# A two-block transformer forward pass on one core: the norm between MLP and attention is applied behind the first four projections

## The reference, cut to what matters

```python
# end of the first block
u = rms_norm(h, norm_mlp_pre[l])
f = jnp.square(jax.nn.relu(u @ w_mlp_in[l])) @ w_mlp_out[l]
h = h + rms_norm(f, norm_mlp_post[l])
# start of the second block, i = 0; x is h, ctx are 256 context tokens
hx = modulate(rms_norm_2(x, norm_g[i]), shift_x[:, None], scale_x[:, None])
hc = modulate(rms_norm_2(ctx, norm_g[i]), shift_c, scale_c)
#   rms_norm_2(x, g) = x * rsqrt(mean(x * x) + eps) * g;  modulate(h, shift, scale) = h * (1 + scale) + shift
qx, kx, vx, gx = split(hx @ w_in)       # w_in: 1024 -> 4 * 1024, 8 heads of 128
qc, kc, vc, gc = split(hc @ w_in)
qx = rope_axial(qx, ang_r, ang_c); kx = rope_axial(kx, ang_r, ang_c)
# per head: softmax(q1 k1) - lam * softmax(q2 k2), times v; then a norm, times silu(g)
```

## Time and profile before

| | us |
|---|---|
| median of 3 runs | 1629.29 (1629.1 to 1634.57) |
| the profiled execution, its own time | 1629.36 |
| its span in the profile | 1627.2 |
| outside the span | 2.16 |
| PE busy | 1556.7 (96% of the span) |
| DVE, ACT, POOL busy | 985.8, 751.7, 504.6 |
| mean granted clock of TensorE | 0.984 of full |

### The profile page before, as it was taken

The page is one execution under the profiler, slowest core; times in us unless marked ns, Lnnn a source line. Parts: engine busy times, 40 slices in busy tenths (PEclk is TensorE's granted clock), DMA queues, the critical chain, the costliest instruction groups (busy, mean ns, idle before and its releaser), DMA issues.

```text
span 1627.2 us, 23677 instructions
## 1 busy us (share of the span) xinstructions
PE 1556.7 (96%) x8392; PEld 1221.3 (75%) x8392; DVE 985.8 (61%) x2266; ACT 751.7 (46%) x1413; POOL 504.6 (31%) x231
## 2 busy tenths in 40 slices
PE   7998999999899999999899999999999989999997
PEld 5886666678688888888877877778777768876566
DVE  6235555355679867645666666675676267147854
ACT  6225766634342423234344554455445343248753
POOL 3651232245244444444221111121214354230012
PEclk9999999999999999999899999999999989999999
DMA  6861112264356565643111111111111122220001
GB/s 200 174 162 33 59 59 77 76 256 130 104 193 194 191 198 188 198 134 100 53 53 39 40 39 39 39 39 39 39 39 52 52 56 89 78 66 14 2 14 65
DMA packets 48401, 149.34 MB, mean 92 GB/s; under 512 B 5782, under 2 KB 9110, under 8 KB 48184
## 3 DMA queue, kind: packets, MB, share of 16 engines
q1 hardware_dynamic: 37080, 112.45, 23.0%
q10 hardware_dynamic: 11232, 35.72, 6.8%
HBM read 141.53 MB, written 6.62 MB: 91 GB/s over the span
## 4 chain that ended last, share of the span: by engine, by line
PE 80%; DVE 7%; ACT 5%; issue 5%; POOL 1%; DMA 1%; ACTq 0%; POOLq 0%; DVEq 0%; SPq 0%
PE ps L347 41%; PE ps L351 20%; PE ps L570 4%; PE ps L581 3%; PE ps L551 3%; PE ps L1347 3%; PE ps L1311 2%; PE ps L1323 1%; POOL w_l L973 1%; PE ps L415 1%; PE ps L1075 1%; ACT sb L636 1%; DVE tg L1921 1%; ACT w_h L330 1%; DVE b_sb L675 1%
## 5 line engine op out<-in xcount | busy, mean ns | idle before, releaser
L973 POOL TENSOR_TENSOR w_l<-raw,w_h 128x1024 fp32r<-128x1024 f32 (+1 forms) x190 | 457.0, 2406 | 897.1 <-ACT w_h L330 877.4
L330 ACT ACTIVATE w_h<-raw 128x1024 fp32r<-128x1024 f32 x190 | 200.7, 1058 | 360.5 <-PE ps L347 305.3
L347 PE MATMUL ps<-x2h,w_h 128*128 128x512 f32 (+1 forms) x816 | 245.3, 366 | 19.5 <-DVE x2l L1994 7.6
L347 PE MATMUL ps<-x1h,w_h 128*128 128x512 f32 x584 | 237.9, 407 | 16.0 <-POOL w_l L973 10.4
L347 PE MATMUL ps<-x2h,w_l 128*128 128x512 f32 (+1 forms) x816 | 231.8, 349 | 0.0
L351 PE MATMUL ps<-x2l,w_h 128*128 128x512 f32 (+1 forms) x816 | 231.7, 349 | 0.0
L347 PE MATMUL ps<-x1h,w_l 128*128 128x512 f32 x584 | 230.7, 395 | 0.0
L351 PE MATMUL ps<-x1l,w_h 128*128 128x512 f32 x584 | 230.1, 394 | 0.0
L347 PEld LDWEIGHTS ps<-x2h,w_h 128*128 128x128 f32 x816 | 132.4, 191 | 52.6 <-issue 17.1
L347 PEld LDWEIGHTS ps<-x2h,w_l 128*128 128x128 f32 x816 | 132.2, 191 | 20.8
L351 PEld LDWEIGHTS ps<-x2l,w_h 128*128 128x128 f32 x816 | 132.5, 191 | 19.5
(11 more groups left out here) (318 smaller groups left out, 2615.3 us busy)
## 6 DMA issues: line engine op xcount, KB each, us to landing
raw<-in_w_mlp SPq DMA_DIRECT2D x64, 512.0 KB, 3.7
mraw<-in_w_mod ACTq DMA_DIRECT2D x51, 512.0 KB, 3.7
raw<-in_w_a SPq DMA_DIRECT2D x32, 512.0 KB, 3.6
raw<-in_w_att SPq DMA_DIRECT2D x25, 512.0 KB, 11.3
raw<-in_w_b SPq DMA_DIRECT2D x20, 512.0 KB, 3.6
raw<-in_w_g SPq DMA_DIRECT2D x16, 512.0 KB, 3.6
raw<-in_w_ao SPq DMA_DIRECT2D x9, 512.0 KB, 3.5
gates<-g_stage ACTq DMA_DIRECT2D x16, 256.0 KB, 2.2
```

The lines of the kernel that those rows point to most:

```text
L330: nc.scalar.activation(split(u)[0], raw[:, u % RAW], ACT.Copy).then_inc(w_hi, 1)
L347: mm = nc.tensor.matmul(o, w[:, k], xh(k), start=(first and k == k0 and wi == 0), stop=(last and k == k1 - 1 and wi == 1))
L973: nc.gpsimd.tensor_tensor(l[:, ks], raw[:, u % RAW, ks], h[:, ks].bitcast(F32), ALU.subtract).then_inc(w_lo, 1)
```

## The change

Head 0's four projections are made from tiles of the residual stream that are multiplied by gain and scale only; the token's norm factor is applied to the finished PSUM banks, and the shift, which the norm factor doesn't touch, is added as a column.

- `x2h`/`x2l` get four more columns (SCX = SC + 4). Columns SC and SC+1 hold the two shift vectors, so `first_ctx` runs over C + 2 = 258 columns and its bank's column C is weight x shift. Addresses behind them move by a quarter KB.
- DVE's scale, add and low half of the unnormalised tile run together (`g_scale`, `g_add`, `g_low`), as in the kernel's norm ahead of the MLP (L1953, L1960, L1965). ACT rounds each tile to `xph` ahead of squaring it.
- PE: four k-tiles of context products of U_A between the steps of the first norm, the rest behind its spread, then all of U_A+1. Then for each of 8 tiles the column sums and the products of both units over the latent tokens. Then U_A+2: half, the second norm's spread, the other half, its context; then U_A+3, context and latent.
- U_A+2's weight has a third slot (`w_h4`/`w_l4`, over `m_l`), split behind the MLP, ahead of the first norm's root. U_A+3's weight is split behind the second spread, U_A+4's within the shifts at k = 3, U_A+5's behind the gate's tanh.
- DVE (`evict_first`) scales the shift column and multiplies the bank by the norm factor; ACT (`take_first`) copies with scale and bias. Units 0 and 1 come ahead of `modulated`, which still makes `x2h`/`x2l` of the latent tokens for heads 1 to 7; units 2 and 3 behind it, and the first rotation behind those.
- `project((None, 0), ...)` is gone. Head 0 begins with `dense(9)`, and its later `dense` calls are smaller by 9 in sum. The gate is finished between the two rotations.

```diff
@@ lows, POOL: U_A to U_A+3 written out, then the loop @@
-            lows(U_A, U_AO + 1)
+            for u in range(U_A, U_A + 4):
+                low(u)
+            lows(U_A + 4, U_AO + 1)
@@ tensor @@
             nm3a.wait(pe, "add", KT - 1)
             column_sums(sqsum, 4, S, True, False)
+            pe.wait_ge(ml_f, 4 + N_MLP - 2)
+            first_ctx(0, 1, 0, 2)
             nm3a.wait(pe, "sq", KT)
             column_sums(sq[:, 1], 4, S, False, True).then_inc(nm3a.mm, 1)
+            first_ctx(0, 1, 2, 4)
             nm3a.wait(pe, "rc", 1)
             nm3c.wait(pe, "lo", KT)
             spread(5, 0, 4).then_inc(nm3a.r, 1)
+            first_ctx(0, 1, 4, KT)
             pe.wait_ge(ml_f, 4 + N_MLP)
-            first_ctx(0, 0, KT)
-            tile_sum(0)
-            first_ctx(1, 0, KT // 2)
-            tile_sum(1)
-            first_ctx(1, KT // 2, KT)
-            for k in range(2, KT):
+            first_ctx(1, 3, 0, KT)
+            for k in range(KT):
                 tile_sum(k)
+                nm3p.wait(pe, "lo", k + 1)
+                for j in range(2):
+                    mm = first_x(j, 2 * j, k, k + 1)
+                    if k == KT - 1:
+                        mm.then_inc(unit, 1)
+            first_x(2, 4, 0, 4)
             nm3b.wait(pe, "rc", 1)
             spread(7, 0, 4).then_inc(nm3b.r, 1)
-            for k in range(KT + LAG):
...
+            first_x(2, 4, 4, KT)
+            nm3b.wait(pe, "src", KT)
+            first_ctx(2, 5, 0, KT).then_inc(unit, 1)
+            first_ctx(3, 6, 0, KT)
+            wait_head(pe, "k", (None, 0), 1, 1)
+            first_x(3, 2, 0, KT).then_inc(unit, 1)
...
+                    if i is None and j == 0:
+                        nm3b.wait(pe, "lo", k + 1)
...
+                lead = i is None and c == 0
+                if lead:
+                    dense(9)
+                    wait_head(pe, "g", head, 1, 1)
                 wait_head(pe, "ro", head, 2, 2)
                 scores(0)
-                dense(2 if more else 3)
+                dense(1 if lead else 2 if more else 3)
...
-                dense(4 if more else 3)
+                dense(2 if lead else 4 if more else 3)
                 for qt in range(4):
                     scores(qt + 2)
-                    dense(2 if more else 4 + (qt == 0))
+                    dense(1 if lead else 2 if more else 4 + (qt == 0))
                     turns(qt)
-                    dense(1 + qt % 2 if more else 3)
+                    dense(1 + qt // 2 if lead else 1 + qt % 2 if more else 3)
                 turns(4)
-                dense(4)
+                dense(2 if lead else 4)
...
-            project((None, 0), 2 * KT, 2 * KT)
             pe.wait_ge(ha["ones"], 1)
             all_heads(pe, attend)
@@ scalar @@
             mlp(3, False, True)
+            split_high(act, U_A + 2)
...
                 nm3b.wait(act, "src", k + 1)
+                nc.scalar.activation(xph[:, k, :], hc[:, k, 0:S], ACT.Copy, scale=mulx[:, 0, 0, k:k + 1]).then_inc(nm3p.hi, 1)
...
+            nm3b.wait(act, "r", 1)
+            nc.scalar.activation(rstd[:, 0:S], ps[:, 7], ACT.Copy).then_inc(n3_r, 1)
+            split_high(act, U_A + 3)
+            def take_first(j, dst, scale):
+                wait_head(act, "em", (None, 0), 8, 2 * j + 2)
+                nc.scalar.activation(dst[:, S:SC], ps[:, 2 * j + 1, 0:C], ACT.Copy, scale=scale)
+                return nc.scalar.activation(dst[:, 0:S], ps[:, 2 * j], ACT.Identity, bias=shifted[:, j:j + 1], scale=scale)
+            take_first(0, a_q, -0.125).then_inc(ha["q"], 1)
+            take_first(1, a_k, 1.0).then_inc(ha["k"], 1)
             for k in range(KT):
                 nm3b.wait(act, "t", k + 1)
-                shift_tile(k, 0, xn3, 0).then_inc(nm3b.hi, 1)
+                shift_tile(k, 0, xn2, 0).then_inc(nm3b.hi, 1)
+                if k == 3:
+                    split_high(act, U_A + 4)
             nc.scalar.activation(dev[:, 6:7], eps_t, ACT.Tanh)
+            take_first(2, a_vT, 1.0).then_inc(ha["v"], 1)
...
+            split_high(act, U_A + 5)
...
+                if lead:
+                    wait_head(act, "ro", head, 2, 1)
+                    take((None, 1), 0, True)
@@ vector @@
+            def evict_first(j, bank, ctx_bank, scale):
+                unit_done(v, U_A + j)
+                nc.vector.tensor_scalar(shifted[:, j:j + 1], ps[:, ctx_bank, C:C + 1], scale, None, ALU.mult).then_inc(ha["em"], 1)
+                nc.vector.tensor_tensor(ps[:, bank], ps[:, bank], rstd[:, 0:S], ALU.mult).then_inc(ha["em"], 1)
             invert(v, nm3b, S)
-            modulated(nm3b, 0, xn3, (0,))
+            v.wait_ge(n3_r, 1)
+            evict_first(0, 0, 1, -0.125)
+            evict_first(1, 2, 3, 1.0)
+            modulated(nm3b, 0, xn2, (0,))
+            evict_first(2, 4, 5, 1.0)
+            unit_done(v, U_A + 3)
+            done(nc.vector.tensor_copy(shifted[:, 3:4], ps[:, 6, C:C + 1]))
+            nc.vector.tensor_tensor(ps[:, 2], ps[:, 2], rstd[:, 0:S], ALU.mult).then_inc(ha["em"], 1)
+            settle(v)
+            wait_head(v, "em", (None, 0), 8, 7)
+            nc.vector.tensor_scalar(ps[:, 2], ps[:, 2], shifted[:, 3:4], None, ALU.add).then_inc(ha["em"], 1)
             v.wait_ge(tab_in, 32)
...
             rotate((None, 0), 0, "q")
+            wait_head(v, "gt", (None, 0), 1, 1)
...
             rotate((None, 0), 1, "k")
             nc.vector.tensor_copy(ones_r[:], ones[:]).then_inc(ha["ones"], 1)
-            gate_up((None, 0))
             all_heads(v, attend)
```

More of the change, by code:

```diff
@@ L327, in split_high @@
                     act.wait_ge(up_free, 4)
+            elif i is None and u == U_A + 2:
+                act.wait_ge(unit, U_A)
             else:
@@ L445, in build @@
         n3_sum = sem("n3_sum")
+        n3_r = sem("n3_r")
         fin_g = sem("fin_g")
@@ L1177, in _, with first_ctx, first_x, tile_sum @@
             mlp(3, range(8, 16))
+            def first_ctx(j, bank, k0, k1):
+                split_ready(pe, U_A + j)
+                return products(U_A + j, [(ps[:, bank, 0:C + 2], lambda k: x2h[:, k, S:SC + 2], lambda k: x2l[:, k, S:SC + 2])],
+                                k0, k1, first=(k0 == 0), last=(k1 == KT),
+                                ready=(lambda k: nm3c.wait(pe, "lo", k + 1)) if j == 0 else None)
+            def first_x(j, bank, k0, k1):
+                split_ready(pe, U_A + j)
+                return products(U_A + j, [(ps[:, bank], lambda k: xph[:, k, :], lambda k: xpl[:, k, :])], k0, k1,
+                                first=(k0 == 0), last=(k1 == KT))
+            def tile_sum(k):
+                nm3b.wait(pe, "sq", k + 1)
+                column_sums(sq[:, k % 2], 6, S, k == 0, k == KT - 1).then_inc(n3_sum, 1)
             nm3a.wait(pe, "add", KT - 1)
             column_sums(sqsum, 4, S, True, False)
+            pe.wait_ge(ml_f, 4 + N_MLP - 2)
+            first_ctx(0, 1, 0, 2)
             nm3a.wait(pe, "sq", KT)
             column_sums(sq[:, 1], 4, S, False, True).then_inc(nm3a.mm, 1)
+            first_ctx(0, 1, 2, 4)
             nm3a.wait(pe, "rc", 1)
@@ L1230, in project @@
                         split_ready(pe, u, i, 8)
-                        if i is not None or c:
+                        if i is None and j == 0:
+                            wait_head(pe, "q", (None, 0), 1, 1)
+                        else:
                             wait_head(pe, "gqkv"[j], head, 1, 1 if j else 0)
[L1234 to L1238, removed]
+                    if i is None and j == 0:
+                        nm3b.wait(pe, "lo", k + 1)
+                    mm = products(u, [(ps[:, 0], lambda k: x2h[:, k, 0:S], lambda k: x2l[:, k, 0:S]),
+                                      (ps[:, 1, 0:C], lambda k: x2h[:, k, S:SC], lambda k: x2l[:, k, S:SC])],
                                   k, k + 1, first=(k == 0), last=(k == KT - 1))
@@ L1590, in take @@
                 unit_done(act, U_A + 4 * c + j, i, 8)
[L1591 to L1594, removed]
+                src = pair(0)[:, 0:SC]
                 if j == 0:
@@ L1602, in take @@
                     nc.scalar.activation(a_g[c % 2][:], src, ACT.Tanh, scale=0.5).then_inc(ha["gt"], 1)
-                if ahead and (j == 3 or not begins):
+                if ahead:
                     split_high(act, U_A + 4 * c + j + 2, i, 8)
@@ L1663, in attend @@
                 exps(1, 1)
-                if more:
+                if more and not lead:
                     take((i, c + 1), 0, True)
-                else:
+                elif not more:
                     take_out(0)
@@ L1688, in attend @@
                     take_out(6)
-            for j in range(4):
-                take((None, 0), j, True)
             all_heads(act, attend)
```

95 lines of the change are left out of this document (56 added, 39 removed).

## The result

| | kernel before | changed kernel |
|---|---|---|
| median | 1630.67 us (1629.10 to 1634.57, 7 runs) | 1639.14 us (1638.40 to 1641.54, 7 runs) |
| profiled execution, its span | 1627.2 us | 1639.8 us (its own time 1641.54) |
| mean granted clock | 0.984 | 0.981 |

The changed kernel is slower: the ratio is 1.005, 95% interval 1.0037 to 1.0064, or 8.5 us between the medians. The interval excludes no change, but not the 0.5% that the forecast named as the least that can be told from it. The three runs known when the prediction was made had a median of 1629.29.

The account below looks back on a forecast made before the run. PE was taken as the bound, 80% of the chain. The terms put head 1's scores at 907.9 against 899.3, +8.6 us on 1629.36: 1638.0 us (+0.53%), range 1632 to 1645.

Parts of the forecast that it names:

- the seam: From the first column sums behind the MLP to head 1's scores; the forecast put their start 8.6 us later.
- the chain on DVE: From the second spread (through at 819.4) over low halves, evictions and rotations to `ones_r`, forecast at 850.1.
- the way to head 0's scores: Behind `ones_r`: `dense(9)` 9.5, half-clock loss 2.5, wait for ACT's eviction 1.1; 13.1 in all, scores at 863.2.
- The rival that it wouldn't: PE's clock stays at 0.50 in the first norm's filled pauses, all later by 2.9 or twice that: 1641 to 1644; chance 0.2.
- The eight tiles: PE's column sums plus products of units 0 and 1: 2.25 per tile, 18.0 in all, 797.5 to 815.5.
- POOL and DVE: POOL's subtractions delay DVE: 1.7 at the low halves, 2.2 in the rotation of q.
- The wait for `ones`: Ahead of head 0, PE idles from 833.6 to 850.1, 16.5 us, with nine ready k-tiles queued behind the wait.
- k's wait: In head 0, behind query block 4's scores, k-tile 16 waits for head 1's k: 2.4 us (bounds 0.9 and 3).
- The term of 44.7: Head 0's length from its scores to head 1's: 53.3 - 9.5 - 1.5 + 2.4 = 44.7, end at 907.9.
- the third rival: PE passes `ones` before 841.5, nine k-tiles run under the rotations: -4.5, 1624.9, or 1627 with half-clock start; chance 0.1.

Follow-up runs that it names:

- in the second: Second profile of the changed kernel, run again unchanged on the chip of the next three experiments: 1639.69 us, ratio 1.005 to the kernel before.
- the layout run: The kernel before with only the change's layout: `x2h` and `x2l` four columns wider, what lies behind moved by a quarter KB; 1630.06 us, ratio 0.9992.
- the kernel with the later rounding: The changed kernel with U_A+4's rounding at k = 7 of the shifts in place of k = 3; 1637.12 us in a single run.
- the pair: The changed kernel with all edits found, its second spread directly behind the eight tiles (1620.91 us) or back behind half of unit 2 (1623.98 us).
- the kernel of the early `ones_r`: The changed kernel with DVE making `ones_r` right behind the second norm's reciprocal, not behind the rotation of k; 1629.55 us, ratio 0.9989.
- the filled kernel: The kernel before with only U_A's first four k-tiles of context products put into the first norm's two pauses; 1633.41 us, ratio 1.0002.

## Why the prediction was right

The forecast was +8.6 us on 1629.36 (1638.0 us); it came out at 1639.14, 8.5 us over the kernel before. That these two agree within 0.1 us is in part luck. What the sum adds up is the seam, and the seam took 7.6 us more in the first profile and 7.4 in the second; about 1 us of the 8.5 lies outside it, in the scatter that the layout run shows. Within the seam the chain on DVE was 1.4 us early and the way to head 0's scores 0.8 shorter than forecast, against 1.2 more in head 0. The steps themselves came as forecast. Its times can be compared after taking off the 2.4 us by which the profile of the changed kernel starts the seam later.

| step | forecast | measured, less 2.4 |
|---|---|---|
| first spread | 791.75, 1.16 long | 791.64, 1.16 |
| eight tiles begin / end | 797.5 / 815.5 | 797.0 / 815.3 |
| second spread | 818.2 | 818.05 |
| first low half | 823.4 | 823.0 |
| last low half ends | 835.4 | 834.7 |
| rotation of q begins | 837.8 | 836.8 |
| PE starts `dense(9)` | 850.1 | 848.7 |
| head 0's scores | 863.2 | 861.0 |
| head 1's scores | 907.9 | 906.9 |

- **The clock held** through the filled pauses, and through column sums mixed with products: 1.00 in the whole of the first stage. The rival that it wouldn't didn't occur in two of two profiles of the changed kernel, but two of the seven variants with the same program up to there had the first spread at 2.08. So it is a matter of the single execution, and 0.2 was no wrong chance for it. Its price was too high: in those two the second spread came 1.2 us later, where the rival had 2.9.
- **The eight tiles** took 2.29 each against 2.25.
- **POOL and DVE** met where I put them: 1.36 at the low half (1.7 forecast), 2.1 in q's rotation (2.2). The Trainium skill's rule in "SBUF — State Buffer", "Who interferes with whom", sorts the rows rightly: a low half with two SBUF inputs waited for POOL, and the scaling of a bank, with one SBUF and one PSUM input, did not: in the kernel with the later rounding it took 0.69 at 833.34, inside a subtraction that ran from 832.92 for 2.34. But the number of SBUF inputs isn't all: in the kernel before, the cast of q to its high half, with one input, took 2.63 at 830.74 beside a subtraction begun at 830.42, where that of k took 0.56. The experiment with the later rounding, a single run, shows the first of the two as a cause: 1.1 us of `ones_r`'s lateness.
- **The wait for `ones`**, which the whole forecast hangs on, is shown from both sides: one instruction earlier on DVE, or the wait later on PE, takes 10 us off the median.
- **Head 0.** k's wait was 2.3 us (2.4 forecast). I left out that the clock can fall behind it: in the first profile six transposes behind the wait took 1.40 where they take 0.82, and head 0's stage has 0.96. The term of 44.7 was too small by 1.2 in the first profile, and 0.4 too large in the second (44.3), in which the half clock fell on `dense(9)` instead (13.7 in place of 12.3).
- **What the sum didn't have right:** that DVE's chain is a row of terms that add. The forecast says that everything behind the second spread hangs on it; the pair shows that of 2.7 us 2.2 are lost on the way. The forecast itself did not need that step, since it moved nothing there, but an improvement built on it would have been over-estimated fivefold. The remark on the third rival, -4.5 us if nine k-tiles ran under the rotations, was also too good: the kernel of the early `ones_r` had its scores at 62.9 and not at 62.4 us, and a head 0 of 46.7 and not 44.7, and came out at -1.5 in the medians.

## What to carry to other kernels

A wait that has always been passed early is a free choice of place only as long as what stands ahead of it covers it. When ready work is moved behind such a wait, move the wait to the first reader, or its producer to where it has nothing ahead of it; look for it in PE's waits, where one line held 15.7 us. Filling pauses with products is no gain by itself: twelve products stood in the same pauses in the changed kernel, where the clock held behind them, and in the kernel before with that part alone, where they gave nothing. There the work behind the spread ran out sooner; that this is why is likely from its one profile, not shown.

## What the runs showed of the hardware

- The granted clock fell while PE was shown busy without a gap, on column sums alone: in the kernel with only the layout PE was busy for all of 796.70 to 808.39, at 1.00 up to 804, and at 0.50 from 805 on, inside 48 column-sum matmuls that took 7.09 us. In the filled kernel it was already at 0.50 when they began and stayed there for all 10.23 us of them. In between products, in the changed kernel, they ran at 1.00.
- The same instructions up to the first norm gave its spread 1.16 us in seven profiles and 2.08 in two. The second spread came 1.2 us later for that reason alone, so edits of that size are read from a chain of rows, not from a median.
- Two engines that meet on SBUF turn a delay into a phase: pulling DVE's chain forward by 2.7 us, against subtractions of POOL that came forward by 2.7, 1.8, 0.7 and 0.1, cost 2.2 of it.
